# Differential attention in a two-layer trunk: half of the value projection's products issued inside the attention steps, and each head's squares taken in one operation and summed by rows

## The reference

```python
q, k, v = split(h @ w_in, 3)          # 8 heads; q and k have 2 halves of 64, v has 128
q, k = rope(q), rope(k)               # latent tokens only
p = softmax(q k^T)                    # per head and half; context rows see context only
a = p[half 0] - lam * p[half 1]
o = a @ v
o = rms(o) * subln_g * (1 - lam_init) # per head, over its 128 columns
out = concat(o) @ w_out
```

## Time and profile before

| | |
|---|---|
| median of 3 runs | 1889.93 us (1889.65 to 1890.08) |
| the profiled execution | 1891.57 us |
| its span in the trace | 1889.8 us |
| TensorE busy | 1844.6 us, 98% |
| VectorE, ScalarE, GpSimd busy | 1188.3, 688.1, 163.7 us |
| mean granted TensorE clock | 0.992 |
| `diff_v` on TensorE | 493.1 to 541.5 us |
| `diff_attn` on TensorE | 541.5 to 618 us |

### The profile page before, as it was taken

The page is one execution under the profiler, slowest core; times in us unless marked ns, Lnnn a source line. Parts: engine busy times, 40 slices in busy tenths (PEclk is TensorE's granted clock), DMA queues, the critical chain, the costliest instruction groups (busy, mean ns, idle before and its releaser), DMA issues.

```text
span 1889.8 us, 27442 instructions
## 1 busy us (share of the span) xinstructions
PE 1844.6 (98%) x9984; PEld 1583.3 (84%) x9984; DVE 1188.3 (63%) x1890; ACT 688.1 (36%) x1152; POOL 163.7 (9%) x236
## 2 busy tenths in 40 slices
PE   8999999999989999999999999999998999989997
PEld 6888888898966888888889888888897899978886
DVE  7877772355478478777424787753358555667764
ACT  4332232232358242322223323222244333545542
POOL 0010100100301201001000110100102000010000
PEclk9999999999999999999999999999999999989998
DMA  8466643335420146656332566633343222545554
GB/s 322 151 205 196 193 153 108 93 104 161 134 67 1 67 134 209 191 189 189 96 105 90 178 211 189 199 119 92 94 142 123 68 88 90 191 144 186 191 167 124
DMA packets 81886, 271.85 MB, mean 144 GB/s; under 512 B 9489, under 2 KB 14865, under 8 KB 81809
## 3 DMA queue, kind: packets, MB, share of 16 engines
q1 hardware_dynamic: 62354, 201.58, 32.6%
q0 software_dynamic: 19456, 69.22, 12.3%
HBM read 267.62 MB, written 1.05 MB: 142 GB/s over the span
## 4 chain that ended last, share of the span: by engine, by line
PE 88%; DVE 7%; issue 2%; ACT 2%; DMA 0%; POOL 0%; SPq 0%; POOLq 0%; DVEq 0%; ACTq 0%
PE pt L1432 19%; PE pt L1433 19%; PE pt L1435 19%; PE pt L1407 9%; PE pt L1406 4%; PE pt L1627 2%; DVE wl L867 2%; PE pt L1842 2%; PE pt L1844 2%; PE pt L1843 2%; PE pt L1631 1%; PE pt L1505 1%; PE pt L1726 1%; PE pt L1727 1%; PE pt L1728 1%
## 5 line engine op out<-in xcount | busy, mean ns | idle before, releaser
L867 DVE TENSOR_TENSOR wl<-raw,wh 128x1024 fp32r<-128x1024 f32 (+2 forms) x394 | 435.7, 1145 | 410.9 <-ACT wh L578 407.0
L1432 PE MATMUL pt<-xh,wh 128*128 128x512 f32 (+1 forms) x1312 | 495.4, 378 | 0.2 <-DVE wl L867 0.2
L1433 PE MATMUL pt<-xh,wl 128*128 128x512 f32 (+1 forms) x1312 | 494.2, 377 | 0.0
L1435 PE MATMUL pt<-xl,wh 128*128 128x512 f32 (+1 forms) x1312 | 492.9, 377 | 0.0
L578 ACT CAST wh<-raw 128x1024 fp32r<-128x1024 f32 (+2 forms) x394 | 364.0, 970 | 273.3 <-PE pt L1435 148.9
L879 DVE CUSTOM_DVE_ANT_0 pt<-modw,raw 128x1024 f32<-128x1024 f32 x256 | 305.8, 1255 | 15.6 <-DMA modw<-in_mod_rows 15.5
L1432 PEld LDWEIGHTS pt<-xh,wh 128*128 128x128 f32 x1312 | 247.9, 189 | 45.3 <-issue 0.3
L1435 PEld LDWEIGHTS pt<-xl,wh 128*128 128x128 f32 x1312 | 247.7, 189 | 45.0
L1433 PEld LDWEIGHTS pt<-xh,wl 128*128 128x128 f32 x1312 | 247.8, 189 | 44.5
L727 ACT CAST uh<-tmp 128x512 f32 (+3 forms) x88 | 49.8, 568 | 291.9 <-DVE tmp L1171 283.4
L1432 PE MATMUL pt<-uh,wh 128*128 128x512 f32 x396 | 154.0, 389 | 0.0
(11 more groups left out here) (222 smaller groups left out, 2786.4 us busy)
## 6 DMA issues: line engine op xcount, KB each, us to landing
raw<-in_ffn_w SPq DMA_DIRECT2D x238, 512.0 KB, 4.0
modw<-in_mod_rows POOLq DMA_DIRECT2D x128, 512.0 KB, 4.6
raw<-in_ret_w_in SPq DMA_DIRECT2D x48, 512.0 KB, 4.4
raw<-in_diff_w_in SPq DMA_DIRECT2D x24, 512.0 KB, 4.4
raw<-in_ffn_w SPq DMA_DIRECT2D x32, 256.0 KB, 3.9
raw<-in_ret_w_out SPq DMA_DIRECT2D x16, 512.0 KB, 4.1
region<-in_mod_rows SPq DMA_DIRECT2D x8, 512.0 KB, 14.4
region<-in_mod_start SPq DMA_DIRECT2D x8, 512.0 KB, 15.0
```

The lines of the kernel that those rows point to most:

```text
L867: nc.vector.tensor_tensor(flat(wl[:, s, cut]), raw[:, raw_slot(late, s, p), 0:part_rows * CW], flat(wh[:, s, cut].bitcast(F32)), ALU.subtr ...
L1432: nc.tensor.matmul(bank, w_hi[:, k, cut], hi(k), start=a, stop=False)
L1433: nc.tensor.matmul(bank, w_lo[:, k, cut], hi(k), start=False, stop=False)
L1435: return nc.tensor.matmul(bank, w_hi[:, k, cut], lo(k), start=False, stop=b)
```

## The change

- `diff_v` keeps two chunks (value columns 0 to 511, heads 0 to 3). The other two are made inside `diff_attn`, by `fill`: four quarters of 48 matmuls (two token blocks of a chunk), in steps 1 to 4, 6 to 13, 15 to 21 and 23 to 29, right after the score of the step, all in bank 6. ScalarE copies each quarter out in step 5, 14, 22, 30 (`filled`). The next quarter's first fill waits for that copy; the values of heads 4 and 6 wait for their columns.
- All heads' values now use bank 5. The values of an even unit move to step 7 + 4h and wait for the scaling of the head before; those of the odd unit are in step 8 + 4h.
- `square_o` is one operation over 512 columns, first in ScalarE's step 9 + 4h. VectorE adds it by rows (`tensor_reduce`) ahead of the mean, in step 9 + 4h; scaling is in step 10 + 4h, `hi_o`, `lo_o` and `turn_head` in 13 + 4h.
- Rotations go in the order q0, k0, q1, k1, ...: eight in `diff_v`, two ahead of the second maximum, six in steps 6, 8, ..., 16. A head's first score waits for its two rotations. Swaps are issued pair by pair as `qk` is copied out, into a buffer of their own.
- The casts of the last values chunk stay in step 4; those of the output projection's first two chunks are in steps 15 and 32 (low parts 16 and 33). The finished heads go to `head_out`, which lies over `qk`, since `xh` and `xl` are still read by the fills.

```diff
-AT_SQUARE, AT_HI = TURN_LAG + 5, TURN_LAG + 10
-AT_MEAN, AT_SCALE, AT_LO = TURN_LAG + 6, TURN_LAG + 7, TURN_LAG + 10
-AT_TURN = TURN_LAG + 10
+AT_VALUES = (TURN_LAG + 3, TURN_LAG + 4)
+AT_SQUARE, AT_HI = TURN_LAG + 5, TURN_LAG + 9
+AT_MEAN, AT_SCALE, AT_LO = TURN_LAG + 5, TURN_LAG + 6, TURN_LAG + 9
+AT_TURN = TURN_LAG + 9
 V_STEPS = 4 * (DH - 1) + AT_HI + 1
+
+FILL = 2 * DT
+FILL_STEPS = ((1, (4, 4, 4, 4)), (6, (2,) * 8), (15, (3, 2, 2, 2, 2, 2, 3)), (23, (3, 2, 2, 2, 2, 2, 3)))
+AT_FILLED = {5: 0, 14: 1, 22: 2, 30: 3}
+AT_SPLIT, AT_REST = {4: (-1, 1), 15: (0, 0), 32: (0, 1)}, {4: (-1, 1), 16: (0, 0), 33: (0, 1)}
+ROPE_ORDER = [r for h in range(DH) for r in (h, DH + h)]
+ROPES_FIRST = 8
+AT_ROPE = {6 + 2 * n: ROPES_FIRST + 2 + n for n in range(6)}
...
+            head_out = sb("head_out", [P, 2 * DH, TOK], F32R, where=g)
...
-        other_rows = part(2 * DH, LAT, at=taken[0] - 2 * LAT - 2 * TT * LAT - 4 * TOK)
+        other_rows = part(2 * DH, LAT)
...
-                    for s in range(2):
-                        pool.wait_ge(evac[s], 2 * (ph["sa"], ph["sb"])[s])
                     n = DD // 4
                     for g in range(4):
+                        for s in range(2):
+                            pool.wait_ge(evac[s], 2 * ((ph["sa"], ph["sb"])[s] - 3 + g))
...
+                    for s in range(2):
+                        for b in range(2):
+                            tile_done(s0[s], s, b, 2 * q0 + s)
+                            nc.scalar.copy(vd[:, 2 * b:2 * b + 2, s * CW:(s + 1) * CW],
+                                           pt[:, 2 * s + b, :].rearrange("p (a c) -> p a c", a=2)).then_inc(evac[s], 1)
+                            if s == 1 and b == 0:
+                                exps(0, 0)
+                        if s == 0:
+                            split(q0 + 1, 0, late=late)
...
+                    def filled(f):
+
+                        s, b = divmod(f, 2)
+                        tile_done((values["sa"], values["sb"])[s] + 1, s, b, 2 * (values["q"] + 1) + s)
+                        nc.scalar.copy(vd[:, 2 * b:2 * b + 2, (2 + s) * CW:(3 + s) * CW],
+                                       pt[:, 6, :].rearrange("p (a c) -> p a c", a=2)).then_inc(evac[s], 1)
                     def square_o(h):
                         act.wait_ge(pv_done, 2 * h + 2)
-                        if h >= 2:
-                            act.wait_ge(hvar_ready, h - 1)
-
-                        for b in range(TT):
-                            at = TT * (h % 2) + b
-                            nc.scalar.activation(tmp[:, 0, b * P:(b + 1) * P], pt[:, 5 + h % 2, b * P:(b + 1) * P], ACT.Square,
-                                                 accum_out=o_sums[:, at:at + 1]).then_inc(o_squared, 1)
+                        if h:
+                            act.wait_ge(o_summed, h)
+                        nc.scalar.activation(tmp[:, 0, :], pt[:, 5, :], ACT.Square).then_inc(o_squared, 1)
                     def hi_o(h):
                         act.wait_ge(o_turned, h + 1)
-                        nc.scalar.activation(xh[:, h, :], pt[:, SUM, :], ACT.Copy, scale=subg).then_inc(o_hi, 1)
+                        nc.scalar.activation(head_out[:, h, :], pt[:, SUM, :], ACT.Copy, scale=subg).then_inc(o_hi, 1)
                     for v in range(V_STEPS):
+                        if AT_SQUARE <= v < AT_SQUARE + 4 * DH and (v - AT_SQUARE) % 4 == 0:
+                            square_o((v - AT_SQUARE) // 4)
                         if TURN_LAG <= v < V + TURN_LAG:
                             turn_out((v - TURN_LAG) // 2, (v - TURN_LAG) % 2)
                         if 0 < v < V:
                             exps(v // 2, v % 2)
-                        if v == 4:
-
-                            split(q0, 1, late=late)
-                        for at, step in ((AT_SQUARE, square_o), (AT_HI, hi_o)):
-                            if at <= v < at + 4 * DH and (v - at) % 4 == 0:
-                                step((v - at) // 4)
+                        if v in AT_FILLED:
+                            filled(AT_FILLED[v])
+                        if v in AT_SPLIT:
+                            pair, s = AT_SPLIT[v]
+                            split(q0 + pair, s, late=late)
+                        if AT_HI <= v < AT_HI + 4 * DH and (v - AT_HI) % 4 == 0:
+                            hi_o((v - AT_HI) // 4)
...
+                    def rope(n):
+
+                        r = ROPE_ORDER[n]
+                        tile, other = qk[:, r, 0:LAT], tmp[:, (1, 4)[n % 2], 0:LAT]
                         dve.wait_ge(swap_landed[r // 4], 16 * P * 4 // DD)
-                        nc.vector.tensor_tensor(tmp[:, bank % 2, 0:LAT], other_rows[:, r, :], droped[:, 1], ALU.mult).then_inc(rope_terms, 1)
+                        nc.vector.tensor_tensor(other, other_rows[:, r, :], droped[:, 1], ALU.mult).then_inc(rope_terms, 1)
                         nc.vector.tensor_tensor(tile, tile, droped[:, 0], ALU.mult).then_inc(rope_terms, 1)
-                        dve.wait_ge(rope_terms, 2 * r + 2)
-                        nc.vector.tensor_tensor(tile, tile, tmp[:, bank % 2, 0:LAT], ALU.add).then_inc(roped, 1)
+                        dve.wait_ge(rope_terms, 2 * n + 2)
+                        nc.vector.tensor_tensor(tile, tile, other, ALU.add).then_inc(roped, 1)
                     dve.wait_ge(rope_landed, 16)
                     for s in range(2):
                         dve.wait_ge(evac[s], 2 * s0[s])
-                    for i in range(count):
-                        for s in range(2):
-                            for e in range(4):
-                                rope(8 * i + 4 * s + e, 4 + e, row(qk, 8 * i + 4 * s + e)[:, 0:LAT])
-                            if not (i == count - 1 and s == 1):
-                                rest(2 * (q0 + i + 1) + s, s, late=late)
+                    for n in range(ROPES_FIRST):
+                        if n == ROPES_FIRST - 2:
+                            rest(2 * (q0 + 1), 0, late=late)
+                        rope(n)
...
+                    rope(ROPES_FIRST)
+                    rope(ROPES_FIRST + 1)
                     row_max(0, 1)
                     def mean_o(h):
-                        dve.wait_ge(o_squared, TT * (h + 1))
+                        dve.wait_ge(o_squared, h + 1)
+                        if h >= 2:
+                            dve.wait_ge(hvar_ready, h - 1)
+                        nc.vector.tensor_reduce(o_sums[:, TT * (h % 2):TT * (h % 2 + 1)],
+                                                tmp[:, 0, :].rearrange("p (b d) -> p b d", b=TT), AX.X, ALU.add).then_inc(o_summed, 1)
+                        dve.wait_ge(o_summed, h + 1)
...
-                                                pt[:, 5 + h % 2, :].rearrange("p (b d) -> p b d", b=TT), factors,
+                                                pt[:, 5, :].rearrange("p (b d) -> p b d", b=TT), factors,
...
-                        if v == 4:
-                            rest(2 * q0 + 1, 1)
+                        if v in AT_REST:
+                            pair, s = AT_REST[v]
+                            rest(2 * (q0 + pair) + s, s, late=late)
+                        if v in AT_ROPE:
+                            rope(AT_ROPE[v])
                         for at, step in ((AT_MEAN, mean_o), (AT_SCALE, scale_o), (AT_LO, lo_o)):
...
+                if g == 0 and b == 0:
+                    pe.wait_ge(roped, 2 * (h + 1))
...
+                    for s in range(2):
+                        pe.wait_ge(lo_ready, 2 * (2 * q0 + s + 1))
+                        claim(s, s0[s], 1)
+                        for n in range(TT):
+                            at = pt[:, 2 * s + n // 2, (n % 2) * CW:(n % 2 + 1) * CW]
+                            for k in range(DT):
+                                ins = value_products(at, s, n, k)
+                            if n == 1:
+                                ins.then_inc(first_tile_done[s], 1)
+                            if n == 1 and s == 1:
+
+                                pe.wait_ge(evac[0], 2 * (s0[0] + 1))
+                                score(0, 0)
+                        ins.then_inc(chunk_done, 1)
...
+                    def fill(f, a, b):
+
+                        s, half = divmod(f, 2)
+                        if a == 0:
+                            if half == 0:
+                                pe.wait_ge(lo_ready, 2 * (2 * (before["q"] + 1) + s + 1))
+                            if f:
+                                was, t = divmod(f - 1, 2)
+                                pe.wait_ge(evac[was], 2 * ((before["sa"], before["sb"])[was] + 1) + t + 1)
+                        for i in range(a, b):
+                            n, k = 2 * half + i // DT, i % DT
+                            ins = value_products(pt[:, 6, (n % 2) * CW:(n % 2 + 1) * CW], s, n, k)
+                        if b == FILL:
+                            ins.then_inc((first_tile_done[s], chunk_done)[half], 1)
```

(52 more changed lines are left out.)

29 lines of the change are left out of this document (3 added, 26 removed).

## The result

| | before | after |
|---|---|---|
| median | 1889.85 us (1889.65 to 1890.08, 4 runs) | 1926.49 us (1924.31 to 1926.81, 4 runs) |
| span of the profiled execution | 1889.8 us | 1925.0 us |
| `diff_v` on TensorE, from its first weights to the attention's first score | 493.1 to 541.5 | 493.3 to 518.6 |
| attention on TensorE | 76.4 us | 136.1 us |

The ratio is 1.019, with a 95% interval of 1.0176 to 1.0204: the changed kernel is 36.6 us slower. The forecast was 1910 with a range of 1899 to 1919, so the sign came out and the size did not.

The account below looks back on a forecast made before the run. Taken as bound: TensorE busy nearly throughout, the attention three engines handing work round. Start plus 6.9, six rounds plus 35.9, then plus 1.4, minus 1.6: plus 42.6, less 23.0, about 20 on 1889.9: 1910 us, range 1899 to 1919.

Parts of the forecast that it names:

- (a): Value projection: two of four value chunks leave, 192 matmuls by 0.12 us, minus 23.0 us, all on the path.
- (b): Attention: the same 192 matmuls come back as fills, plus 23.0 us of TensorE time.
- (c): Attention: with one output bank, values wait for the previous head's scaling; 13.98 us a head against 9, hand-overs adding nothing.
- (d): Attention: eight rotations move in; those at steps 10 and 14 add 2.3 us, step 16's with the cast's remainder 2.4.
- (e): Attention: squares in one operation, 1.00 to about 0.6 us on ScalarE; new VectorE row sum 0.7 us a head.
- the ring: Attention: loop TensorE, ScalarE, VectorE from one head's values to the next sets the pace; 1904 to 1915 us, chance 0.62.
- (f): Attention: the next quarter's fills wait for copies of filled quarters, about 3.5 us at step 6, 1.5 at 15 and 23.
- (g): Query and key projection: row swaps issued by GpSimd pair by pair, rotations not late, no cost.
- The last rival: Attention: the clock falls in waits, 1 to 2 us each in one to five heads; 1912 to 1919 us, chance 0.14.
- Faster: Attention: TensorE's queue stays the bound, values find bank 5 free, fills cover 10.2 us of idle; about 1883 us, chance 0.09.
- Cheaper ring: Attention: turns and scores run tighter among fills, 1.1 us less a round; plus 5 to 14 us, middle 1899, chance 0.12.
- what was named ahead: Attention signs: values waiting about 20 us in all, VectorE some 3 us a head for scores, successive heads 14 us apart.

Follow-up runs that it names:

- zero products: Products of zeros ahead of each scaling wait: 18 in the one-bank kernel without fills, 1916.9 us (1928.6 without); 14 in the changed kernel, also before the first quarter's wait, 1918.8.
- both remedies: The changed kernel with 14 products of zeros ahead of the waits and the squares as before (four operations, no row sum on VectorE): 1916.9 us.

## Why the prediction was right in sign and wrong in size

**(a), (b): right.** Projection 25.3 us to the attention's first score, 23.1 less than before, against 23.0; the 192 products returned as fills, six of them in 0.82 us.

**(c): mechanism right, and shown.** One bank against two, with nothing else changed, is 33.6 us. Its sum of 13.98 is some 0.5 short at full clock (13.0 measured against 12.5 without fills). With fills, the rows offer for it values that take 0.2 more behind a wait and fills of 0.82 instead of 0.72 behind a score. Over six rounds that is 3 to 4 us. The hand-overs, which I set at nothing, are not what is missing.

**(d): near in the rounds,** 5.0 us against 4.7 (rotations taken out), though the clock falls at other places in the two kernels, so the agreement is partly luck. Putting all of them first is no way out: it delays the start by 6.3, part of it clock.

**(e): right.** Row sum 0.68 against 0.7, all of it in the ring.

**(f): right.** Waits for filled quarters 3.49, 1.63 and 1.54 against 3.5, 1.5 and 1.5.

**(g): right,** as far as read: no wait for a swap among the attention's waits.

**The last rival: the step that failed.** The forecast's own sum put the clock at nothing. The prediction carried it as a rival only, with a chance of 0.14, "1 to 2 us" a fall, in one to five heads, plus 1.5 to 8. All of these were too small.

- *The price.* I took it from one row, 16 turns behind a long idle. In this ring the wait is followed by 16 value products (+1.9) and a score (+0.95), and every TensorE instruction of a round up to the turn lies in the ring, so nothing absorbs it: 2.8 us for the fall at 554, and near 2 where the score was already at the upper clock (592).
- *The count.* Eight falls, also behind short waits: at 606 the wait was 1.54, after one of 0.59. I had looked only at the long gap of the earlier trace rows.
- *The place.* It was set beside the ring as a rival. It was a consequence of it: if the ring is right, a wait for a scaling comes in nearly every round, and the clock with it.

With these the excess over the forecast sum can be placed, by rows of the changed kernel: the start 3.0 (2.3 of it after the fall at 534, where step 6's fills and turns run at half speed: 535.24 to 540.27 is 5.0 against 2.7), six rounds 10.6 (99.3 against 88.7), seventh to eighth head 1.8, the last values and on 1.5 (4.3 against 2.8, values of 24 at 0.18 each). Together 16.9, and 19.6 + 16.9 = 36.5 of the 36.7 by which the output projection starts later in the traces. Of the 16.9, the sum's shortness at full clock is 3 to 4 by the 13.0 us rounds; rotations and the third head's cast are in the forecast; about 13 are left for the clock. The zero products gave back 11.7 in the kernel without fills. In the changed kernel they gave back 7.7, with two falls left; 2.2 of it came at the start (19.4 us to the first values, where after has 21.7 and the forecast 18.7). So that the clock is a large part of the excess is shown; the exact split is an account, not a measurement.

The Trainium skill, "TensorE: Matmul & The Clock Gate", section "HAM oscillation — how this bites in real kernels", describes a loop in which each burst of matmuls is shorter than the wait behind it, so that every next burst starts at the half clock. The trace agrees in part. The wait and the low clock do come back round after round, with stretches at 0.50 to 0.57 behind waits of 3.3 to 4.9 us. But the section tells of waits for a DMA, and here they are waits for VectorE; and TensorE's work between two waits is longer than the wait here (540.27 to 552.2 against 3.30), and the clock is back at 1.00 before the next. It was cited in the prediction as a risk and then priced by the one long gap.

**The other rivals.** *Faster* needed a round below TensorE's own 11.6; none of the six was (14.7 to 18.4). *Cheaper ring* hoped for shorter turns and scores among fills: a turn was 0.43 to 0.53 and a score 1.06, as before. Against what was named ahead: values waiting near 20 us in all (17.9), the row sum near 0.69 (0.68), a clock under 0.95 for the last rival (0.86) came as stated; VectorE waited 47.7 us for scores over 21 waits, so nearer 6 a head than 3; and 14 between values (14.7 to 18.4) did not come.

**What stays open.** Fills with two banks for the heads were not tried: all eight banks are in use in mid stage. Why the falls in the kernel with both remedies came where they did is not known. Nothing ran measurably faster than the kernel before.

## What to carry to other kernels

Before giving an accumulator bank to other work, walk the loop from its writer through every reader back to the writer: with one bank that loop is the pace (13.0 us a head at full clock with no fills), with two it was 9.5. If such a loop leaves TensorE a wait in every round, count the clock as part of the round, not as an accident beside it: price it on the instructions that stand right behind the wait. A row sum of 0.7 us that, with the squares in one operation, costs nothing measurable beside two banks (0.08%, within noise) costs its length and more in the ring, so test an idea in the structure it will live in.

## What the runs showed of the hardware that was not expected

The clock fell behind waits much shorter than the 4.88 us of the earlier trace rows: at the end of one of 1.54 us at 606, at 575 some 1.4 us after one of 1.92 had ended, and behind the same wait of 1.72 us in one kernel's profile but not in its near twin's. Matmuls of zeros keep the clock up: 18 of them in each wait kept it at 1.00 from 565 to 600 (0.85 without), and adding 126 matmuls made the kernel 11.7 us faster. A plain float32 product of 512 columns took two records of 0.43 us, where in the output projection a product of the reduced operands with as many columns follows the one before after 0.23 (655.22 to 655.45 in the changed kernel).
